# Gathering the first expert's rows ahead of the gather of all rows

## What is computed

```python
# logits -> one group of 4 per token, and in it the 2 best of 8 experts (32 experts in all)
# for each expert e, over the tokens that chose it:
h_e = silu(x_e @ w_exp_gate[e]) * (x_e @ w_exp_up[e])     # 1024 -> 256, twice
y_e = h_e @ w_exp_down[e]                                  # 256 -> 1024
out[token] += weight(token, e) * y_e
```

## Time and profile before

| | us |
|---|---|
| median of 3 runs | 1992.12 |
| lowest, highest | 1991.62, 1996.06 |
| the profiled execution | 1992.81 |
| its span | 1990.9 |
| TensorE busy in it | 1849.2 (93%) |
| mean granted TensorE clock | 0.983 of full |

### The profile page before, as it was taken

How to read it: one execution, slowest core, us unless ns; L and a number is a source line. 1 busy time by engine, 2 the same in 40 slices (tenths; PEclk the granted TensorE clock), 3 DMA queues, 4 the chain that set the end, 5 groups by cost and what they waited for, 6 DMA issues and landing times.

```text
span 1990.9 us, 33082 instructions
## 1 busy us (share of the span) xinstructions
PE 1849.2 (93%) x12610; PEld 1348.9 (68%) x12610; DVE 1035.5 (52%) x2332; ACT 551.4 (28%) x1185; POOL 54.2 (3%) x76
## 2 busy tenths in 40 slices
PE   6999999999987788899999899999999999999998
PEld 4878788757755566554564688887444465788886
DVE  3366573387442223444778877775987326333311
ACT  3343400172130111221570333332000226244310
POOL 0000000000000000000000011111000000000000
PEclk8999999999998899999999999999999999999999
DMA  9444483423459999630204122223764030144441
GB/s 372 177 190 195 185 359 149 169 86 157 197 241 425 421 418 390 258 127 0 85 2 190 64 84 85 84 84 138 306 252 170 2 108 1 50 155 155 165 187 48
DMA packets 38531, 345.07 MB, mean 173 GB/s; under 512 B 4231, under 2 KB 9102, under 8 KB 10382
## 3 DMA queue, kind: packets, MB, share of 16 engines
q1 hardware_dynamic: 37550, 334.02, 42.7%
q10 hardware_dynamic: 864, 9.44, 1.1%
HBM read 380.14 MB, written 1.05 MB: 191 GB/s over the span
## 4 chain that ended last, share of the span: by engine, by line
PE 86%; issue 4%; DVE 4%; DMA 2%; PEld 2%; ACT 1%; DVEq 0%; SPq 0%; PEldq 0%; ACTq 0%
PE bank L672 49%; PE bank L1428 13%; PE bank L1192 5%; PE bank L1177 3%; PE bank L1217 2%; PE bank L793 2%; PEld bank L672 2%; PE bank L1393 1%; PE bank L1302 1%; PE bank L1310 1%; DMA ring<-in_ada 1%; PE bank L1153 1%; PE bank L1400 1%; PE bank L898 1%; DVE ring L2135 1%
## 5 line engine op out<-in xcount | busy, mean ns | idle before, releaser
L672 PE MATMUL bank<-hn,ring 128*128 128x256 f32 (+2 forms) x2080 | 514.3, 407 | 9.8 <-ACT hn L1526 4.6
L672 PE MATMUL bank<-arena,ring 128*128 128x256 f32 (+2 forms) x1600 | 467.3, 449 | 17.8 <-issue 13.9
L672 PEld LDWEIGHTS bank<-hn,ring 128*128 128x128 f32 (+1 forms) x2080 | 395.3, 191 | 119.2 <-issue 68.6
L672 PEld LDWEIGHTS bank<-arena,ring 128*128 128x128 f32 (+1 forms) x1600 | 298.0, 188 | 180.4 <-issue 148.2
L1428 PE MATMUL bank<-ring 128*128 128x256 f32 x704 | 160.7, 381 | 1.2 <-DVE ring L2762 0.6
L1428 PEld LDWEIGHTS bank<-ring 128*128 128x128 f32 x704 | 133.7, 191 | 21.6 <-issue 2.1
L2022 DVE SCALAR_TENSOR_TENSOR bank<-ring,c_rows 128x1024 f32<-128x1024 f32 x96 | 118.1, 1231 | 21.5 <-DMA ring<-in_ada 16.7
L1428 PE MATMUL bank<-hn,ring 128*128 128x256 f32 x528 | 123.0, 383 | 3.8 <-ACT hn L1882 3.8
L2022 DVE SCALAR_TENSOR_TENSOR ring<-ring,c_rows 128x1024 f32<-128x1024 f32 x96 | 117.2, 1221 | 0.0
L1506 ACT ACTIVATE hn<-resid 128x256 f32<-128x256 f32 (+1 forms) x48 | 22.6, 485 | 336.5 <-DVE resid L2113 336.5
L1428 PEld LDWEIGHTS bank<-hn,ring 128*128 128x128 f32 x528 | 101.4, 192 | 18.5 <-issue 4.6
(11 more groups left out here) (434 smaller groups left out, 2072.5 us busy)
## 6 DMA issues: line engine op xcount, KB each, us to landing
ring<-in_ada SPq DMA_DIRECT2D x28, 2048.0 KB, 8.2
ring<-in_up SPq DMA_DIRECT2D x44, 1024.0 KB, 4.8
ring<-in_egu SPq DMA_DIRECT2D x20, 2048.0 KB, 16.3
ring<-in_edn SPq DMA_DIRECT2D x32, 1024.0 KB, 14.2
hn<-in_egu ACTq DMA_DIRECT2D x15, 2048.0 KB
arena<-in_egu SPq DMA_DIRECT2D x11, 2048.0 KB, 13.9
ring<-in_down SPq DMA_DIRECT2D x16, 1408.0 KB, 9.3
ring<-in_adat SPq DMA_DIRECT2D x8, 2048.0 KB, 11.8
```

The costliest lines, as they stand in the source:

```text
L672: last = mm(out, lhs(i), rhs(i), start=i == 0, stop=i == k - 1)
```

## The change

The 32 rows of item 0 are gathered by 16 products of their own (128 stationary columns, 32 moving ones, all into bank 6), ahead of the gather of all rows. ScalarE copies them with one instruction to `x_t[0]`. `step(0)` stands behind the first block (k = 0) of the gather of all, and its silu between ScalarE's copies of k = 2 and k = 3. The gather now starts only when both halves of `pick` are there. Behind the gather, `token_rows` no longer waits for the last copy; the wait for it stands ahead of the small product into bank 5. The counts of `moe_X` and `moe_Xev` are one higher throughout.

```diff
+            pe.wait_ge(s["tok_ev"], 1)
+            pe.wait_ge(s["moe_G"], TT)
+            for k in range(KD):
+                for t in range(TT):
+                    last = mm(bank[6][:, k * CAP:(k + 1) * CAP], h_tok[:, t, k * P:(k + 1) * P], pick[:, t, 0:CAP],
+                              start=t == 0, stop=t == TT - 1)
+            last.then_inc(s["moe_X"], 1)
             for k in range(KD):
                 if k >= 4:
-                    pe.wait_ge(s["moe_Xev"], k - 3)
+                    pe.wait_ge(s["moe_Xev"], k - 2)
+                if k == 1:
+                    step(0)
                 for t in range(TT):
-                    if k == 0:
-                        pe.wait_ge(s["moe_G"], t + 1)
                     last = mm(bank[2 + k % 4][:, :], h_tok[:, t, k * P:(k + 1) * P], pick[:, t, :], start=t == 0, stop=t == TT - 1)
...
-            pe.wait_ge(s["moe_Xev"], KD)
-            step(0)
             pe.wait_ge(s["route_dve"], 5)
             token_rows()
+            pe.wait_ge(s["moe_Xev"], KD + 1)
             mm(bank[5][:, 0:4 * OVER], ones[0:NE, :], table[0:NE, :], start=True, stop=True).then_inc(s["route_pe"], 1)
...
+            act_e.wait_ge(s["moe_X"], 1)
+            fn(x_t[0], bank[6][:, 0:KD * CAP].rearrange("p (k x) -> p k x", k=KD), ACT.Copy).then_inc(s["moe_Xev"], 1)
             for k in range(KD):
...
+                if k == 3:
+                    act_e.wait_ge(s["moe_h"], 1)
+                    fn(hsil[:, 0, :], bank[0][:, 0:64], ACT.Silu).then_inc(s["moe_silu"], 1)
-                act_e.wait_ge(s["moe_X"], k + 1)
+                act_e.wait_ge(s["moe_X"], k + 2)
                 fn(xs[:, k, 0:NPOS], bank[2 + k % 4][:, :], ACT.Copy).then_inc(s["moe_Xev"], 1)
```

More of the change, by code:

```diff
@@ L1144, in _ @@
             mm(bank[7][0:NE, NE + 1:NE + 2], sel_both, ones[:, 0:1], start=True, stop=True).then_inc(s["route_pe"], 1)
-            pe.wait_ge(s["tok_ev"], 1)
-            for k in range(KD):
-                if k >= 4:
-                    pe.wait_ge(s["moe_Xev"], k - 3)
-                for t in range(TT):
-                    if k == 0:
-                        pe.wait_ge(s["moe_G"], t + 1)
[L1153 to L1158, removed]
-            pe.wait_ge(s["moe_Xev"], KD)
[L1161 to L1168, removed]
             def combine(v):
@@ L1184, in step @@
                     x = i % 2
-                    if i >= 1:
+                    if i == 0:
+                        pe.wait_ge(s["moe_Xev"], 1)
+                    else:
                         pe.wait_ge(s["moe_xt"], i)
@@ L1191, in step @@
                         for q in range(4):
-                            last = mm(bank[x][CAP * q:CAP * q + CAP, 0:P], x_t[x][:, k, :] if i else xs[:, k, 0:CAP],
+                            last = mm(bank[x][CAP * q:CAP * q + CAP, 0:P], x_t[x][:, k, :],
                                       w_gate_up(BUFFER[i])[:, k * 512 + q * P:k * 512 + (q + 1) * P],
@@ L1219, in step, with token_rows @@
                     last.then_inc(s["moe_y"], 1)
-            step(0)
+            pe.wait_ge(s["tok_ev"], 1)
[5 more added lines that the diff above has]
+            last.then_inc(s["moe_X"], 1)
+            for k in range(KD):
+                if k >= 4:
+                    pe.wait_ge(s["moe_Xev"], k - 2)
+                if k == 1:
+                    step(0)
+                for t in range(TT):
+                    last = mm(bank[2 + k % 4][:, :], h_tok[:, t, k * P:(k + 1) * P], pick[:, t, :], start=t == 0, stop=t == TT - 1)
+                last.then_inc(s["moe_X"], 1)
+                if k == 4:
+                    pe.wait_ge(s["route_dve"], 4)
+                    mm(bank[7][0:NE, NE + 2:NE + 3], C("trix", NE)[:, 0:NE], cnt[0:NE, 1:2], start=True, stop=True) \
+                        .then_inc(s["route_pe"], 1)
+            def token_rows():
+                for b, pair in ((6, (pos_a, pos_b)), (7, (t2b, t2c))):
+                    for x, value in enumerate(pair):
+                        for t in range(TT):
+                            last = mm(bank[b][:, x * T + t * P:x * T + (t + 1) * P], value[:, t, 0:1].to_broadcast([P, P]), ident,
+                                      start=True, stop=True)
+                last.then_inc(s["moe_rows"], 1)
             pe.wait_ge(s["route_dve"], 5)
             token_rows()
+            pe.wait_ge(s["moe_Xev"], KD + 1)
             mm(bank[5][:, 0:4 * OVER], ones[0:NE, :], table[0:NE, :], start=True, stop=True).then_inc(s["route_pe"], 1)
@@ L1778, in _ @@
                         act_e.wait_ge(s["moe_he"], i - 1)
[L1779 removed]
+                    if i > 0:
+                        fn(hsil[:, i % 2, :], bank[i % 2][:, 0:64], ACT.Silu).then_inc(s["moe_silu"], 1)
                     if i in next_over:
```

2 lines of the change are left out of this document (1 added, 1 removed).

## The result

| | us |
|---|---|
| kernel before, median of 7 runs | 1996.06 (1991.62 to 2001.47) |
| changed kernel, median of 7 runs | 2003.18 (1999.92 to 2006.41) |
| ratio | 1.0034, 95% interval 1.0022 to 1.0046 |
| span of the profiled execution | 2001.4, before 1990.9 |

The changed kernel is slower by 0.34%: in us, 6.8, with an interval of 4.4 to 9.2 (the ratio less 1, times 1996). The forecast was slower by 5.8 us. The difference holds, but the time itself, 2003.2, lies above the range given, 1993.8 to 2000.2. One execution of the kernel before, of 2228.21 us, ran at a mean granted clock of 0.863 where the others ran at about 0.98, and is left out of every comparison.

A forecast was written before the change was run, and what follows sets the result against it. The kernel was taken as bound by TensorE's path to the first free buffers, the weight stream, then TensorE. Step 1's end at 596.5 less 585.73 less 4.95 gave +5.8 us; 1992.1 + 5.8 = 1997.9 us, range 1993.8 to 2000.2.

The forecast's parts named there:

- Median: 1992.1 + 5.8: Whole kernel: the forecast shift added to the earlier median, giving 1997.9 us, slower by 0.29%.
- The chain: Experts' stage: TensorE's path to the first free buffers, then the weight stream until 682, then TensorE to the end.
- the balance: Weight stream: shift is step 1's new end less 585.73 less 4.95; the change pays only if that end precedes 590.7.
- the rival in which it absorbs the delay: Weight stream: it is not what step 17 waits for, or item 4's early load frees more; 0 to +2 us, 6%.
- The gain of 4.95 us: Weight stream: item 4's 2048 KB travel in idle time, taking at most 4.95 us off the stream.
- The price of the small products: Item 0's gather: 32 new instructions, 0.212 us each at half clock, 6.8 us; 3.5 at full clock.
- the first rival: Item 0's gather: the clock comes back early, during the small products; +2.6 us, 1994.7, chance 16%.
- the second: Full gather: the clock comes back late, half clock lasting 3.4 us longer over 512-column products; +7.5 us, 1999.6, chance 8%.
- The clock: TensorE: half clock through all 32 new instructions and 3.4 us of the full gather, its first block.
- The start: Item 0's gather: its first small product starts at 567.7, where the third instruction was loaded before.
- What hid the rest: ScalarE's extra copy, table load and item 0's silu fall between gather copies; TensorE does not wait; at most 1 us if uncovered.
- The instruction blocks: TensorE: 64 more instructions shift where instruction blocks are fetched; between 0 and 1 us, either way.

The follow-up runs named there:

- held_load: The changed kernel, but item 4's weight load is issued only when step 1 has ended; ratio 1.0063 (+12.6 us) to the kernel before.
- free_rows: The changed kernel without item 0's own gather, step 0 working on copied token columns (output wrong); ratio 1.0001 (+0.2 us) to the kernel before.
- again: The changed kernel unaltered, measured once more; +8.4 us against the kernel before.
- warm_after: The changed kernel plus 8 products of 512 columns on constants in TensorE's waits for the router and `pick`; ratio 1.0022 (+4.4 us) to the kernel before.
- wide: The changed kernel with item 0's gather streaming 128 columns of `pick` instead of 32; ratio 1.0015 (+3.0 us) to the kernel before.
- behind_two: The changed kernel with item 0's gather behind the first two blocks of the full gather, step 0 behind the third; ratio 1.0017 to the kernel before.
- shift: The kernel before plus 32 tiny products while TensorE waits for the router; ratio 1.0011 (+2.2 us) to the kernel before.

## Why the prediction was right and wrong

**Outside the range: the step "Median: 1992.1 + 5.8".** The shift was added to the median of three runs, and the range was built around it from the rivals alone, with a term of its own for chance that was too small: "The forecast's own spread is 1.5 us". The median of three was low. With 7 to 32 runs the kernel before has medians of 1994.6 to 1996.3, and its executions spread from 1991.3 to 2001.5. The forecast time was 5.3 us short (1997.9 against 2003.2). Of these 3.9 are the base (1996.06 less 1992.12), and 1.3 the shift (7.1 between the two medians, against 5.8). The base alone carries the time past the range: the same shift on 1996.06 gives 2001.9. The three runs shown, 1991.62 to 1996.06, held the warning: their own spread of 4.4 us was nearly as large as the shift, and the highest was where the median later came to lie. It belonged in the range.

**The chain: right.** Step 17 moved by 7.0 us, as the two issues say, and it follows the balance within 1.1 us in all fourteen profiles. `held_load` shows that the stream has no slack, so the rival in which it absorbs the delay falls; `free_rows` shows that item 5's issue is what counts. From step 17 to the end the stretches differ between executions by several us (157.0 to 162.2 to the end of the stage, 1148.7 to 1152.9 behind it), for which the forecast allowed 1.5.

**The gain of 4.95 us: right** as a bound on what the stream loses; `held_load` measured 4.2 beside `again`, and 5.0 in the traces. That only 0.7 us of it is a gain against the kernel before, which the balance said, agrees with `free_rows`, whose interval goes up to a gain of 1.8.

**The price of the small products: right.** 32 x 0.212 = 6.8 us was forecast, 7.0 measured at half clock (6.8 from its start to that of the next row), 3.65 at full, and 3.94 in `warm_after`, where the last two ran into the fall. From the first small product to the start of step 1 it takes 26.8 us (568.81 to 595.62), exactly what was forecast (567.7 to 594.5). The nearest row, 80 columns at half clock, was the right one to take. The page's 107 ns per load (the Trainium skill, TensorE: Matmul & The Clock Gate, "LDWEIGHTS (loading the stationary operand)") holds at full clock (0.11) and not at half (0.21). By its figure the sum would be an estimated 5.8 - 3.4 = +2.4 us; that is near the first rival's +2.6, not near the second's, as the prediction has it.

**The clock: right.** It stayed at half through all of them and the first block behind. The rival of an early rise fell in the profile itself, and `wide` shows on what it hung: with 128 columns the clock does rise within them. That rival's time, 1994.7, was its own +2.6 above the base, and `wide` measured +3.0 (0.8 to 5.0). The rival of a late rise fell as well: step 0, behind the first block, took 1.96 us, at full clock. The measured time lies above this rival's 1999.6 only because of the base.

**The start: 0.7 us short.** I took 567.7 for the first small product, 11.5 behind `iota`; it was loaded at 568.78, 12.2 behind. In the changed kernel's execution the clock was at half already for the small router products ahead of it (L1139 to L1144), as in `wide` and `behind_two`. The profile of the kernel before had them at full clock. `again`, the same program as the changed kernel, had them at full clock too, and its first weight load stood at 568.23, 11.5 behind `iota`, as forecast; its stream moved by 6.1. So the forecast was of the one case, and which of the two an execution meets is chance.

**What hid the rest: right.** ScalarE's copy took 0.38 us, its table load and silu fell between the copies of the gather; TensorE waited for no bank.

**The instruction blocks: perhaps too small.** "Between 0 and 1 us, either way" is the term for 64 more instructions; no trace here shows the fetching of instructions itself. `shift` measured 2.2 (0.4 to 4.0) for 128 in idle time. Half of that on top of the stream's 6.1 to 6.6 would make 7.2 to 7.7 us, between the two measurements of the changed kernel (6.8 and 8.4), but their intervals hold the stream's shift alone as well.

## What to carry to other kernels

Moving a load forward gains at most the part of its transfer that still lay behind the issue of the next load, the one that can't move: put the two issues side by side, and count what is inserted ahead of the second. In this kernel an early product of few columns cost what its weights cost, at the clock of that moment, and the clock stayed low over the dense work behind it; a wider product was the cheaper one (6.04 us against 7.01). A forecast of a time by a small shift needs the spread of the base's executions in its range, not only the bounds of the shift: here three runs spread by 4.4 us, and the shift was 5.8.

## What the runs showed of the hardware

- Back-to-back products with 128x128 weights and 32 moving columns left the clock at half over 7.0 us without a gap (four profiles), and in `warm_after` a full clock fell behind 3.3 us of them; with 128 columns, in `wide`, the clock rose after 4.7 us. In `behind_two` the full clock survived 3.65 us of 32-column products.
- A float32 128x128 weight load followed another in 0.11 us at full clock and 0.21 at half, with 32 moving columns behind each, and at half clock in 0.21 with 128 too.
- The same program gave different stretches: behind the experts' stage 1149.2 and 1151.2 us in two profiles of the kernel before, 1148.7 to 1152.9 in all fourteen, where its code is the same.
- 64 matrix instructions and their loads placed in idle time moved neither of the two issues that the stream begins with, and yet went with +2.2 us (0.4 to 4.0). The cause stays open.
